# FFN up-projection by seven block products instead of eight, with the sums of the X blocks formed by identity products in PSUM

## What is computed

```python
def conv_ffn(x, w_in, b_in, conv_w, conv_b, w_out, b_out):
    h = x @ w_in + b_in                     # w_in is 1024 x 5632
    hp = jnp.pad(h, ((0, 0), (1, 1), (0, 0)))
    h = hp[:, :-2] * conv_w[0] + hp[:, 1:-1] * conv_w[1] + hp[:, 2:] * conv_w[2] + conv_b
    u, g = jnp.split(h, 2, axis=-1)
    return (u * jax.nn.gelu(g, approximate=False)) @ w_out + b_out   # w_out is 2816 x 1024
...
    x = layer_norm(alpha * x + ff, ln_g[i, 1], ln_b[i, 1])
```

## Time and profile before

| | |
|---|---|
| median of three runs | 2929.44 us |
| the profiled execution | 2936.39 us, its span 2934.6 us |
| granted TensorE clock, mean | 0.972 |
| TensorE matmul busy | 2766.2 us, 94% of the span, 13387 matmuls |
| VectorE, ScalarE, GpSimd busy | 1644.1, 993.6 and 1244.3 us |
| FFN stages | 799.5 to about 1551 us and 2193.3 to 2934.6 us |

### The profile page before, as it was taken

How to read it: one execution, slowest core, us unless ns; L and a number is a source line. 1 busy time by engine, 2 the same in 40 slices (tenths; PEclk the granted TensorE clock), 3 DMA queues, 4 the chain that set the end, 5 groups by cost and what they waited for, 6 DMA issues and landing times. The chain is left out here.

```text
span 2934.6 us, 36448 instructions
## 1 busy us (share of the span) xinstructions
PE 2766.2 (94%) x13387; PEld 2303.8 (79%) x13387; DVE 1644.1 (56%) x2106; ACT 993.6 (34%) x1402; POOL 1244.3 (42%) x890
## 2 busy tenths in 40 slices
PE   7999999977899999999998999998789999999998
PEld 6788888866788888888877888887668888888886
DVE  3676666663664444444473777777466444444446
ACT  3545554542231111221223555555323111222222
POOL 2444444323472333333354566654356233332335
PEclk9999999978999999999999999998899999999999
DMA  3100001225021111111121221211602111111111
GB/s 112 31 22 29 29 29 30 55 63 199 22 66 44 43 57 50 43 50 50 43 86 43 55 60 42 50 44 22 213 22 66 43 43 55 52 43 50 50 43 72
DMA packets 212649, 163.16 MB, mean 56 GB/s; under 512 B 34939, under 2 KB 194251, under 8 KB 212555
## 3 DMA queue, kind: packets, MB, share of 16 engines
q1 hardware_dynamic: 212411, 161.38, 18.6%
q10 hardware_dynamic: 144, 0.52, 0.0%
HBM read 137.24 MB, written 24.64 MB: 55 GB/s over the span
## 5 line engine op out<-in xcount | busy, mean ns | idle before, releaser
L1131 PE MATMUL ff_ph<-XTh,WH 128*128 128x512 f32 x1408 | 550.1, 391 | 6.8 <-PEq L41 6.8
L1131 PE MATMUL ff_ph<-XTl,WH 128*128 128x512 f32 x1408 | 549.3, 390 | 0.0
L1131 PE MATMUL ff_ph<-XTh,WL 128*128 128x512 f32 x1408 | 549.2, 390 | 0.0
L1289 DVE SCALAR_TENSOR_TENSOR ff_C<-ff_H,ff_par,ff_C 128x1024 f32<-128x1024 f32 x88 | 206.2, 2344 | 548.3 <-ACT ff_C L1233 548.3
L1069 POOL TENSOR_SCALAR WH<-raw_weights 128x1024 fp32r<-128x1024 f32 x128 | 142.2, 1111 | 847.1 <-PE ff_ph L1131 490.1
L1071 POOL TENSOR_TENSOR WL<-raw_weights,WH 128x1024 fp32r<-128x1024 f32 x128 | 328.7, 2568 | 10.7
L1131 PEld LDWEIGHTS ff_ph<-XTh,WH 128*128 128x128 f32 x1408 | 265.3, 188 | 62.7 <-issue 7.6
L1131 PEld LDWEIGHTS ff_ph<-XTh,WL 128*128 128x128 f32 x1408 | 265.2, 188 | 55.5
L1131 PEld LDWEIGHTS ff_ph<-XTl,WH 128*128 128x128 f32 x1408 | 265.4, 189 | 55.1
L1229 ACT ACTIVATE ff_H<-ff_ph,ff_par 128x1024 f32<-128x1024 f32 x88 | 98.4, 1118 | 553.7 <-PE ff_ph L1131 553.7
L1282 DVE TENSOR_TENSOR X<-ff_po,X 128x512 f32<-128x512 f32 x288 | 191.6, 684 | 102.5 <-PE ff_po L1145 102.5
(11 more groups left out here) (224 smaller groups left out, 5993.4 us busy)
## 6 DMA issues: line engine op xcount, KB each, us to landing
raw_weights<-in_ffn_w_in SPq DMA_DIRECT2D x88, 512.0 KB, 3.8
raw_weights<-in_ffn_w_out SPq DMA_DIRECT2D x44, 512.0 KB, 3.6
raw_weights<-in_attn_w_qkv SPq DMA_DIRECT2D x24, 512.0 KB
raw_weights<-in_na_w_qkv SPq DMA_DIRECT2D x24, 512.0 KB, 4.4
wo_oraw<-heads_t SPq DMA_DIRECT2D x16, 512.0 KB, 4.4
rpb_rows<-da_rows SPq DMA_DIRECT2D x2, 3840.0 KB, 26.7
na_B<-rpb_rows SPq DMA_DIRECT2D x32, 224.0 KB, 4.3
da_E<-in_x SPq DMA_DIRECT2D x8, 512.0 KB, 5.7
```

Source lines behind the costliest of these rows:

```text
L1131: last = nc.tensor.matmul(out[:, at], wt[:, slot, k * P:(k + 1) * P], x[:, k, at], start=(k == 0 and n == 0), stop=(k == KT - 1 and n == 2))
L1289: nc.vector.scalar_tensor_tensor(out=c, in0=h[:, 0:S], scalar=tap[1], in1=c, op0=ALU.mult, op1=ALU.add).then_inc(conv_link, 1)
```

## The change

The up-projection of a hidden tile is seen as a product of 2 x 2 blocks: the parities (u, g) x the halves k = 1, 2 of the width, times the halves k of the width x the halves t = 1, 2 of the positions. Eight block products of 12 matmuls (4 blocks of the width x 3 parts) become the seven of Strassen's scheme (M1 to M7). This is done for tiles 1 to 21; tile 0 keeps the plain form (up_plain, 96 matmuls).

- Of the positions: five sums or differences of quarters of X (B1, B3, B4, B7, B6) are formed once per layer by mix: identity matrices plus and minus as the stationary operand, high and low parts of both quarters as the moving one, 16 matmuls of 128x512 per mix into po; ScalarE copies out the high part (mix_copy) and VectorE the low part (mix_lower). B1, B3 and B4 stand ahead of the plain tile, B7 behind it, and B6 inside tile 1.
- Of the weights: per hidden tile GpSimd forms five sums of quarters of the two weight tiles (quad_add, 128x512). Each of the seven stationary operands is then split: high part by ScalarE (quad_copy), low part by GpSimd (quad_lower, 128x512). They lie in four slots, and a slot is free when the product four places back has been made. The down weights are split likewise (down_copy on ScalarE, down_lower on GpSimd, 128x1024), behind the quarters of the same tile. The loops of split with its TENSOR_SCALAR are gone. The weights come as four pieces of 256 KB per tile.
- Of the results: ScalarE keeps M5 and M2 in SBUF (keep), and VectorE puts H together in eight operations of 128x512 per tile, each of a PSUM and an SBUF operand: sum_u (two), cross_take, main_prepare and main_take (two each). The middle tap is now made from H in SBUF (centre_tap). The taps, the product and its low part are as they were.
- The order: tiles 2, 4, ... 18 are each followed by a down phase; a tile's taps are worked off inside the next tile (odd tiles) or inside the down phase (even tiles up to 18). Loops are unrolled.
- output_stage puts its two split tiles into slots 6 and 7; the rows of the norm's gain and bias lie in WH and are loaded later.

```diff
+    PLAIN = 1
+    NS = FT - PLAIN
+    GROUPS = FT // 2 - 2
...
+    SLOTS = 4
+    M5, M2, M1, M3, M4, M7, M6 = range(7)
+    SUMS = {M5: 1, M2: 2, M1: 3, M7: 4, M6: 5}
+    B1, B3, B4, B7, B6 = range(5)
...
+        def d_slot(f):
+            if f < FT - 2:
+                return WDh[:, f % 2], WDl[:, f % 2], WDf[:, f % 2]
+            return WH[:, f - FT + 2], WL[:, f - FT + 2], wraw[:, f - FT + 2]
...
+        quarter = {(k, t): (block_of(XTh, k, t), block_of(XTl, k, t)) for k in (1, 2) for t in (1, 2)}
+        mixes = {B1: (quarter[1, 1], quarter[2, 2], plus, (kept_block(WH, 2), kept_block(WL, 2))),
+                 B3: (quarter[1, 2], quarter[2, 2], minus, (kept_block(WH, 4), kept_block(WL, 4))),
+                 B4: (quarter[2, 1], quarter[1, 1], minus, (kept_block(WH, 0), kept_block(WL, 0))),
+                 B7: (quarter[2, 1], quarter[2, 2], plus, quarter[2, 1]),
+                 B6: (quarter[1, 2], quarter[1, 1], plus, quarter[1, 2])}
+        moving = {M5: quarter[2, 2], M2: quarter[1, 1], M1: mixes[B1][3], M3: mixes[B3][3], M4: mixes[B4][3],
+                  M7: quarter[2, 1], M6: quarter[1, 2]}
...
+            def piece(f, gate, k):
+                n = f - PLAIN
+                if n:
+                    sp.wait_ge(quad_sum, 5 * (n - 1) + (5 if k == 1 else 4))
+                    if gate == 0 and k == 1:
+                        sp.wait_ge(quad_low, index(f - 1, M3) + 1)
+                    if gate == 1 and k == 2:
+                        sp.wait_ge(quad_low, index(f - 1, M4) + 1)
+                src = column_tile(w_in_d, f * P + gate * FF)[:, (k - 1) * HK:k * HK]
+                sp.dma_start(quad(gate, k).rearrange("p (k n) -> p k n", k=HK), src).then_inc(piece_in[2 * gate + k - 1], 16)
...
+            def pieces(f):
+                piece(f, 0, 2)
+                piece(f, 1, 2)
+                piece(f, 0, 1)
+                piece(f, 1, 1)
...
+            def down(f):
...
+                elif f < FT - 2:
+                    sp.wait_ge(down_done, OUTS * (f // 2))
+                else:
+                    sp.wait_ge(quad_sum, 5 * NS)
...
+            pieces(PLAIN)
...
-            def split(w, uses, raw_slot, slot):
-
-                pool.wait_ge(wt_in[raw_slot], 16 * (uses - 1))
-                if not (isinstance(w, int) and w == CUT):
-                    hold(pool, w_low, w - CUT, pool_passed)
-                nc.gpsimd.tensor_scalar(wh[:, slot], wraw[:, raw_slot], 1.0, 1.0, ALU.mult, ALU.mult).then_inc(w_high, 1)
-                pool.wait_ge(w_high, w + 1 - CUT)
-                nc.gpsimd.tensor_tensor(out=wl[:, slot], in0=wraw[:, raw_slot], in1=wh[:, slot].bitcast(F32),
-                                        op=ALU.subtract).then_inc(w_low, 1)
...
+            def quad_add(f, j):
+                n, i = f - PLAIN, index(f, j)
+                a, b, op = {M5: ((0, 1), (0, 2), ALU.add), M2: ((1, 1), (1, 2), ALU.add), M1: ((0, 1), (1, 2), ALU.add),
+                            M7: ((0, 2), (1, 2), ALU.subtract), M6: ((1, 1), (0, 1), ALU.subtract)}[j]
+                for gate, k in (a, b):
+                    pool.wait_ge(piece_in[2 * gate + k - 1], 16 * (n + 1))
+                if i >= SLOTS:
+                    pool.wait_ge(made, i - SLOTS + 1)
+                nc.gpsimd.tensor_tensor(out=Rf[:, i % SLOTS], in0=quad(*a), in1=quad(*b), op=op).then_inc(quad_sum, 1)
...
+            def quad_lower(f, j):
...
+                i = index(f, j)
+                pool.wait_ge(quad_high, i + 1)
+                src = quad(0, 1) if j == M3 else quad(1, 2) if j == M4 else Rf[:, i % SLOTS]
+                nc.gpsimd.tensor_tensor(out=Rl[:, i % SLOTS], in0=src, in1=Rh[:, i % SLOTS].bitcast(F32),
+                                        op=ALU.subtract).then_inc(quad_low, 1)
+            def down_lower(f):
+                pool.wait_ge(down_high, f + 1)
+                high, low, full = d_slot(f)
+                nc.gpsimd.tensor_tensor(out=low, in0=full, in1=high.bitcast(F32),
+                                        op=ALU.subtract).then_inc(down_low, 1)
+            def next_quads(f):
+                quad_add(f, M5)
+                quad_add(f, M2)
+                quad_lower(f, M5)
+                quad_add(f, M1)
+                quad_lower(f, M2)
+                quad_lower(f, M1)
+                quad_lower(f, M3)
...
+            for f in range(PLAIN, FT):
+                quad_lower(f, M4)
+                quad_add(f, M7)
+                quad_add(f, M6)
+                quad_lower(f, M7)
+                quad_lower(f, M6)
+                down_lower(f - 1)
+                if f + 1 < FT:
+                    next_quads(f + 1)
...
+            def mix(c):
+                a, b, sign, _ = mixes[c]
+                for half in range(2):
+                    n = 2 * c + half
+                    if n >= 2:
+                        pe.wait_ge(mix_low, n - 1)
+                    for i in range(2):
+                        for j, (w, x) in enumerate(((plus, a[0]), (plus, a[1]), (sign, b[0]), (sign, b[1]))):
+                            last = nc.tensor.matmul(po[:, 2 * half + i], w[:], x[:, 2 * half + i], start=(j == 0), stop=(j == 3))
...
+            def multiply(f, j, out):
+                i = index(f, j)
+                pe.wait_ge(quad_low, i + 1)
+                xh, xl = moving[j]
+                for k in range(HK):
+                    wh, wl = (part[:, i % SLOTS, k * P:(k + 1) * P] for part in (Rh, Rl))
+                    for n, (w, x) in enumerate(((wh, xh), (wh, xl), (wl, xh))):
+                        last = nc.tensor.matmul(out, w, x[:, k], start=(k == 0 and n == 0),
...
+            def up_seven(f):
+                n = f - PLAIN
+                if n:
+                    pe.wait_ge(cross_h, 2 * n - 1)
+                else:
+                    pe.wait_ge(up_out, 2 * PLAIN)
+                multiply(f, M5, P12)
+                if n:
+                    pe.wait_ge(cross_h, 2 * n)
+                multiply(f, M2, P21)
+                if n:
+                    pe.wait_ge(main_h, 2 * n - 1)
+                else:
+                    mix(B6)
+                    pe.wait_ge(mix_low, 2 * B1 + 2)
+                multiply(f, M1, P11)
+                pe.wait_ge(kept, 2 * n + 1)
+                if n == 0:
+                    pe.wait_ge(mix_low, 2 * B3 + 2)
+                multiply(f, M3, P12)
+                pe.wait_ge(kept, 2 * n + 2)
+                if n == 0:
+                    pe.wait_ge(mix_low, 2 * B4 + 2)
+                multiply(f, M4, P21)
+                pe.wait_ge(u_first, n + 1)
+                if n == 0:
+                    pe.wait_ge(mix_low, 2 * B7 + 2)
+                multiply(f, M7, P11)
+                if n:
+                    pe.wait_ge(main_h, 2 * n)
+                else:
+                    pe.wait_ge(mix_low, 2 * B6 + 2)
+                multiply(f, M6, P22)
...
+            for f in range(PLAIN, FT):
+                up_seven(f)
+                if f % 2 == 0 and f < FT - 2:
+                    down(f // 2 - 1)
...
+            def down_copy(f):
+                act.wait_ge(down_in[f % 2], 16 * (f // 2 + 1))
+                high_, _, full = d_slot(f)
+                if f >= FT - 2:
+                    act.wait_ge(made, index(FT - 1, M4) + 1)
+                nc.scalar.activation(high_, full, ACT.Copy).then_inc(down_high, 1)
...
+            def quad_copy(f, j):
...
+            def keep(f, j):
...
+            def centre_tap(f, parity):
+                n, idx = f - PLAIN, f + parity * FT
+                act.wait_ge(a_low, f)
+                act.wait_ge(cross_h, 2 * n + 1 + parity)
+                act.wait_ge(main_h, 2 * n + 1 + parity)
+                nc.scalar.activation(C[:, parity], H[:, parity, 1:S + 1], ACT.Identity, bias=par[:, 4, idx:idx + 1],
...
+            for f in range(PLAIN, FT):
+                behind_down = f % 2 == 1 and 3 <= f < FT - 1
+                if behind_down:
+                    high(f - 1)
+                keep(f, M5)
+                quad_copy(f, M4)
+                keep(f, M2)
+                if f == PLAIN:
+                    mix_copy(B6)
+                quad_copy(f, M7)
+                quad_copy(f, M6)
+                if not behind_down:
+                    gate(f - 1)
+                if f < FT - 1:
+                    down_copy(f - 1)
+                if not behind_down:
+                    high(f - 1)
+                if f + 1 < FT:
+                    quad_copy(f + 1, M5)
+                    quad_copy(f + 1, M2)
+                    quad_copy(f + 1, M1)
+                else:
+                    down_copy(FT - 2)
+                    down_copy(FT - 1)
+                centre_tap(f, 0)
+                if f + 1 < FT:
+                    quad_copy(f + 1, M3)
+                centre_tap(f, 1)
+                if f % 2 == 0 and f < FT - 2:
+                    gate(f)
+            gate(FT - 1)
...
+            def sum_u(f):
+                n = f - PLAIN
```

(64 more changed lines are left out.)

460 lines of the change are left out of this document (241 added, 219 removed).

## The result

The changed kernel takes **2963.32 us** (median of 4 runs, 2960.93 to 2965.84) where the kernel before took 2929.74 (4 runs). The ratio is 1.0114, with an interval of 1.0096 to 1.0131: it is **slower by 1.1%**. The prediction was 2927 us, with faster as the likeliest sign. The time lies inside its range of 2866 to 2966, but the kernel got slower where the sum had it 2.6 us faster. The profiled execution took 2965.84 us against 2936.39 before, 29.4 us more, where the sum had 2.6 less: 32 us are to be explained. From 2927 to the median it is 36; the other 4 are that the profiled execution of before lay 6.95 us over the median of three that the prediction used, and that of after only 2.5 over its own.

What follows compares the result with a forecast made beforehand. TensorE, busy 94%, was taken as the bound. Per layer, rounds -22.3, outside -0.7, mixes +18.1 and start +3.6 us gave -1.3, both layers -2.6; adjusted to the median, 2927 us, range 2866 to 2966.

Steps and rivals of the forecast that it cites:

- The matmuls: On TensorE: 344 fewer; seven products save 57.1 us per layer, the five mixes add 18.1 us.
- The stall: Before down output 4: TensorE waits 3.8 us every round for GpSimd's M1 work, centre_tap, left tap and first addition.
- The durations of GpSimd: 512-column operations take 1.29 us alone, 1.26 in a row; each meeting with VectorE at the port costs GpSimd 1.09 us.
- Rivals 1: Cheaper small GpSimd operations, 1.19 us each, or some meetings missed: 26 us less, 2901 us; chance 0.22.
- rival 3: Each GpSimd operation also pays 0.08 us for a semaphore: 34 us more in the same chain, 2965 us; chance 0.15.
- the prediction's own sign: Distance between down phases: near 60 us means rival 2, 65 us or more means rival 3.
- rival 4: TensorE's clock falls at each 3.8 us stall, 1.7 us each, 31 us in all: 2958 us; chance 0.06.
- Outside the rounds: Per layer: tiles 1, 20 and 21 -8.2 us, tile 21's wait +3.7, tile 2's +2.0, the end +1.8; sum -0.7.
- The wait at the end: Down weights of tiles 20 and 21 split on GpSimd while the last taps run: +1.8 us per layer (0 to 4).
- the start: At the stage's start TensorE waits for plus and minus, +1.9 us; mixes wait for halves of po, +1.7, per layer.
- Rival 2: In the rounds: no stall at all, without the even tile's six meetings; 2852 us; chance 0.10.

Runs made afterwards that it cites:

- the first experiment: The version with the taps first: centre_tap moved ahead of the copies in ScalarE's queue, against the changed kernel; 2875.76 us, ratio 0.9804 to the kernel before.
- the additions first: In the down phases VectorE does the first two additions to X ahead of the left tap, against the changed kernel; 2955.22 us, ratio 1.0072 to the kernel before.
- the filled one: The changed kernel plus 15 unread matmuls between down outputs 3 and 4, where TensorE otherwise pauses; 2939.1 us, ratio 1.0019 to the kernel before.
- the short taps: Left and right taps of tiles 1, 3 to 19 cut to one column, against the changed kernel; 2899.07 us, ratio 0.9887 to the kernel before.

## Why the prediction was wrong

**The matmuls.** Right: 344 fewer, and the 72-matmul stretch at full clock is 16.45 us where 72 x 0.2267 gives 16.3.

**The stall.** Right in place, chain and nearly in size. Product and low part ended 1080.58 us, 19.0 us after the even tile's start at 1061.6 (predicted 19.1), the first addition 28.05 (predicted 28.3), the pause is 3.46 to 3.5 us (predicted 3.8). In the first round of each layer it is 2.67. The 0.2 to 0.3 us less in the others are the sum of small errors in the timetable. That the chain is the one it said is shown by the first experiment, where cutting it takes the whole pause away.

**The durations of GpSimd.** Right. Its 512-column operation takes 1.29 us alone, two in a row 2.54 (predicted 1.26 each; measured 1.27), and where VectorE's operations meet them:

```profile
1057.16 2.54 POOL L1162 TENSOR_TENSOR ff_Rlf<-raw_weights 128x512 f32<-128x512 f32 x2
1072.61 3.54 POOL L1169 TENSOR_TENSOR ff_Rl<-ff_Rlf,ff_Rh 128x512 fp32r<-128x512 f32 x2
1079.45 3.53 POOL L1162 TENSOR_TENSOR ff_Rlf<-raw_weights 128x512 f32<-128x512 f32 x2
1084.19 1.29 POOL L1162 TENSOR_TENSOR ff_Rlf<-raw_weights 128x512 f32<-128x512 f32 x1
```

A pair with a meeting costs 0.99 us more than one without (1.09 less the shortening of 0.15 was 0.94). Rivals 1 and 3, cheaper and dearer operations, both fall: rival 3, at 2965, would give the measured time within 2 us and, by the prediction's own sign (65 us a round; 64.98 measured), would be taken for the cause, and is wrong. That the time lies inside the range is luck: its upper end was this rival's. It asked for operations of 1.35 us and a stall of over 5; what makes the round 65 us is 3.46 of pause and 1.3 to 1.6 of clock.

**The clock: the step that failed.** The sum priced a stall at its length, and rival 4, which had the clock fall at each one, got 0.06. Its price was right: 1.7 us for each fall, 27.3 over 16 measured, and its 2958 is 5 us off. Its dismissal was the error. The prediction read the pause in the earlier trace rows as the end of a mostly idle stretch and put its own "in dense work"; the earlier trace rows was its other evidence, with nine waits that were 0.8 us long and so said nothing of a pause of 3.5. The only row it showed with a pause of that size, 3.83 us, had the lower clock behind it. And the trace of before, outside the rows taken from it, had the case in dense work too: in the attention stage of layer 0 TensorE is busy for 10.7 us at clock 1.00, pauses 3.76 us for GpSimd, and goes on at 0.50 (window, row, window):

```profile
48.00:58.70 10.70, 10.70 (x48) 8.54 (x46) 7.67 (x6) 5.10 (x6) 3.64 (x2) 1.00 0.00 0
62.48 0.77 PE L347 MATMUL da_pa<-XTh,da_wh 128*128 128x512 f32 x1 [3.76 <-POOL da_wl L272]
62.50:65.50 3.00, 3.00 (x7) 2.43 (x8) 0.00 (x0) 0.00 (x0) 2.75 (x2) 0.50 0.60 171
```

What the runs showed in place of "no fall in dense work": the clock fell in 32 of 32 rounds with a pause of 2.96 to 3.5 us (16 of the changed kernel, 16 with the additions first), at 1.7 us a fall, so the term belonged into the sum. When exactly it falls stays open: rival 4's "each" held for 16 of 18 rounds.

**Outside the rounds.** Per layer: tile 21's M5 pause is 3.6 us (predicted 3.7), right. Tile 2's is 2.7 (predicted 2.0). Behind tile 2's the clock fell in both layers (20.76 us for 19.04), behind tile 21's only in layer 0 (21.70); in layer 1 the same pause left it at 1.00, and the tile took 19.49. The wait at the end is 1.65 and 2.3 us (predicted 1.8). The plain tile begins at 816.07 (the prediction's terms give 815.7). TensorE's timeline at tile 2 and its window, granted clock 0.57 behind a pause of 2.7 us:

```profile
866.94 0.47 PE L1241 MATMUL ff_ph<-XTh,ff_Rh 128*128 128x512 f32 x1 [2.54 <-POOL ff_Rl L1169]
867.52 0.63 PE L1241 MATMUL ff_ph<-XTh,ff_Rl 128*128 128x512 f32 x1
```

```profile
867.00:869.90 2.90, 2.90 (x8) 2.29 (x9) 0.04 (x1) 1.84 (x3) 2.90 (x3) 0.57 0.00 0
```

And the row and the window of tile 21 in layer 1:

```profile
2886.47 0.47 PE L1241 MATMUL ff_ph<-XTh,ff_Rh 128*128 128x512 f32 x1 [3.49 <-POOL ff_Rl L1169]
```

```profile
2886.50:2889.50 3.00, 3.00 (x13) 2.49 (x14) 0.10 (x1) 1.90 (x3) 3.00 (x3) 1.00 0.00 0
```

**The missed 32 us together:** clock in the rounds 27.3; tile 2, twice 0.7 of pause and 1.7 of clock, 4.8; tile 21, 2.7 in layer 0, where the clock fell, and 0.4 in layer 1; the end 0.4; the start 0.5; the rounds apart from the clock -2.7 (their pauses are 7.7 us shorter in all than 18 x 3.8, the rest of a round some 0.3 us longer than the count of matmuls). That makes 33.4, 1.4 more than is to be explained. The 28 and 63 us between the changed kernel, the filled one and the one with the taps first bear out the two large terms on the chip; the small ones are read from the trace alone.

**Rival 2,** no stall, was put at 2852 us for a timetable without meetings. The version with the taps first gives 2876 (2872 by its ratio to before) with all meetings in place. The 20 us between are tile 21's pause, 3.7 a layer, the clock behind the pauses of tiles 2 and 21, 1.7 each, and 0.34 us in each of 18 rounds. The missing thing was not a faster GpSimd but a tap that does not queue behind it.

## What to carry over

A pause of TensorE has two prices: its length, and the clock behind it. For pauses of 2 to 4 us, as here, add some 1.6 us to each until rows of the same kernel show otherwise, as an estimate and not a certainty, and search the whole trace for pauses of that length in work of the same kind before setting the term to nothing. When new work fills an engine that was idle, follow every copy that waits for it into its own queue: what stands behind that copy and does not need it should go ahead of it.

## What had not been expected of the hardware

In the FFN stages of all runs, after a pause with dense work on both sides, the granted clock fell to the lower level as follows:

| the pause | how often the clock fell |
|---|---|
| 3.6 to 3.7 us (M5 of tile 21) | 8 of 10 |
| 2.96 to 3.5 us (rounds) | 32 of 32 |
| 2.7 us (M5 of tile 2) | 12 of 12 |
| 2.67 us (first rounds of the changed kernel) | 0 of 2 |
| 2.6 us (rounds) | 12 of 16 |
| 2.2 to 2.3 us (two first rounds, last down phases) | 8 of 10 |
| 1.9 us or less | none, the 18 rounds with the short taps among them |

So from 2.2 to 3.7 us no length divides the two cases. A fall in a round costs 1.3 to 1.8 us, in two rounds of the changed kernel 2.9. Matmuls that do nothing but run through the pause prevent it: 15 of them per round, 3.4 us, bought back 28 us in all. Six meetings with VectorE's two-SBUF operations fall into an even tile, each about 1.0 us of GpSimd's time, and four of them taken away gave back 1.9 us and not 4.4, because a copy or a slot was the next thing waited for.
